# A two-layer hybrid decoder trunk in float32: the GLU projections moved to the head of the layer, the convolution wholly on VectorE, the indexer's head pairs scored one per unit

## The reference

```python
h = rms_norm(x, norm1_g[l])
proj = h @ w_in[l]
q, k, v, iq, ik, iw, glu_in, mq, gates = jnp.split(proj, bounds, axis=-1)
# A: index[q, s] = sum_h iw[h] * relu(iq_h . ik_s); top 64 keys per query; attention of 8 heads over those
# B: a, gte = split(glu_in + conv_in_b); u = a * sigmoid(gte)
#    causal depthwise convolution of u, 31 taps over 512 channels; LayerNorm; silu
# C: 4 heads of cross-attention into 256 memory tokens
merged = g[:, :, 0] * y_attn + g[:, :, 1] * y_mem + g[:, :, 2] * y_conv
x = x + merged @ w_out[l]
x = x + jnp.square(jax.nn.relu(rms_norm(x, norm2_g[l]) @ w_up[l])) @ w_down[l]
```

## Time and profile before

| | |
|---|---|
| Median of three runs | 2966.69 us (2966.26 to 2967.82) |
| The profiled execution's own time | 2967.76 us |
| Its span, first to last instruction | 2966.1 us |
| PE / DVE / ACT / POOL busy | 97% / 59% / 45% / 11% of the span |
| Mean granted clock of PE | 0.996 of full speed |
| Chain that ended last | PE 88%, DVE 5%, of it line 1152 (`conv_acc`) 3% |
| Idle of PE before line 548, released by DVE's `lo` | 37.3 us |
| Steps of the convolution on DVE (line 1152) | 180 of 707 ns mean |
| POOL's two kinds (lines 1578, 1580) | 60 of 1226 ns, 60 of 1057 ns |

### The profile page before, as it was taken

How to read it: one execution, slowest core, us unless ns; L and a number is a source line. 1 busy time by engine, 2 the same in 40 slices (tenths; PEclk the granted TensorE clock), 3 DMA queues, 4 the chain that set the end, 5 groups by cost and what they waited for, 6 DMA issues and landing times.

```text
span 2966.1 us, 38416 instructions
## 1 busy us (share of the span) xinstructions
PE 2891.1 (97%) x13120; PEld 2376.0 (80%) x13120; DVE 1745.2 (59%) x1849; ACT 1347.8 (45%) x1657; POOL 313.6 (11%) x331
## 2 busy tenths in 40 slices
PE   7998999999999999999999989999999999999998
PEld 6876788888888888888878768888888888888887
DVE  4689655556555555545546986555555555555554
ACT  5543644444443444444445446444444434344443
POOL 1158200000000000000020772000000000000000
PEclk9999999999999999999999999999999999999999
DMA  7653556665656556565565444666566565555653
GB/s 268 203 167 128 157 181 202 206 219 199 199 185 198 185 187 195 184 189 188 185 225 171 163 141 154 188 208 231 185 203 201 188 189 186 195 184 186 196 185 128
DMA packets 274090, 558.65 MB, mean 188 GB/s; under 512 B 13168, under 2 KB 13168, under 8 KB 271376
## 3 DMA queue, kind: packets, MB, share of 16 engines
q1 hardware_dynamic: 266384, 523.53, 53.8%
q0 software_dynamic: 5888, 30.02, 3.6%
q10 hardware_dynamic: 1664, 3.15, 0.3%
HBM read 550.37 MB, written 6.29 MB: 188 GB/s over the span
## 4 chain that ended last, share of the span: by engine, by line
PE 88%; DVE 5%; issue 4%; DMA 1%; ACT 1%; DVEq 0%; ACTq 0%; POOL 0%; POOLq 0%; SPq 0%
PE acc L548 28%; PE acc L550 28%; PE acc L549 28%; DVE conv_acc L1152 3%; PE tp L561 3%; DVE lo L1091 1%; ACT hi L818 1%; PE tp L631 1%; DMA conv_bias<-in_conv_o_b 1%; PE sc L615 0%; PE sc L604 0%; DVE index L1170 0%; DMA x_tok<-in_x 0%; DMA raw<-in_w_in 0%; DVE head_sum L1278 0%
## 5 line engine op out<-in xcount | busy, mean ns | idle before, releaser
L1091 DVE TENSOR_TENSOR lo<-raw,hi 128x1024 fp32r<-128x1024 f32 (+1 forms) x1008 | 1239.5, 1232 | 1172.4 <-ACT hi L818 1163.6
L818 ACT ACTIVATE hi<-raw 128x1024 fp32r<-128x1024 f32 (+1 forms) x1008 | 1055.6, 1048 | 1472.3 <-PE acc L550 1468.3
L548 PE MATMUL acc<-hi,hT_hi 128*128 128x512 f32 x2304 | 922.4, 400 | 37.3 <-DVE lo L1091 37.2
L550 PE MATMUL acc<-hi,hT_lo 128*128 128x512 f32 x2304 | 902.2, 392 | 0.0
L549 PE MATMUL acc<-lo,hT_hi 128*128 128x512 f32 x2304 | 901.2, 391 | 0.0
L548 PE MATMUL acc<-hi,bT_hi 128*128 128x512 f32 x1408 | 555.3, 394 | 0.0
L550 PE MATMUL acc<-hi,bT_lo 128*128 128x512 f32 x1408 | 548.9, 390 | 0.0
L549 PE MATMUL acc<-lo,bT_hi 128*128 128x512 f32 x1408 | 548.2, 389 | 0.0
L548 PEld LDWEIGHTS acc<-hi,hT_hi 128*128 128x128 f32 x2304 | 434.8, 189 | 135.6 <-DVE lo L1091 48.5
L550 PEld LDWEIGHTS acc<-hi,hT_lo 128*128 128x128 f32 x2304 | 434.6, 189 | 93.8
L549 PEld LDWEIGHTS acc<-lo,hT_hi 128*128 128x128 f32 x2304 | 435.1, 189 | 86.7
(11 more groups left out here) (224 smaller groups left out, 1641.1 us busy)
## 6 DMA issues: line engine op xcount, KB each, us to landing
raw<-in_w_in SPq DMA_DIRECT2D x160, 1024.0 KB, 5.0
raw<-in_w_up SPq DMA_DIRECT2D x128, 1024.0 KB, 5.3
raw<-in_w_down SPq DMA_DIRECT2D x128, 1024.0 KB, 5.1
raw<-in_w_out SPq DMA_DIRECT2D x32, 1024.0 KB, 5.1
raw<-in_w_mem_kv SPq DMA_DIRECT2D x16, 1024.0 KB, 5.1
raw<-in_w_attn_o SPq DMA_DIRECT2D x16, 1024.0 KB, 5.1
raw<-in_w_conv_o SPq DMA_DIRECT2D x8, 1024.0 KB, 5.0
raw<-in_w_mem_o SPq DMA_DIRECT2D x8, 1024.0 KB, 5.1
```

The costliest lines, as they stand in the source:

```text
L548: pe.matmul(o, a1, w1, start=first and dk == 0, stop=False)
L550: mm = pe.matmul(o, a2, w1, start=False, stop=last and dk == 1)
L818: act.activation(hi[:, u % 4, :, 0:w], raw[:, c, 2 * (u % 2):2 * (u % 2) + 2, 0:w], ACT.Copy).then_inc(hi_ready, 1)
L1091: dve.tensor_tensor(lo[:, u % 4, :, 0:w], raw[:, u // 2, 2 * (u % 2):2 * (u % 2) + 2, 0:w], hi[:, u % 4, :, 0:w].bitcast(F32), ALU.subtrac ...
```

## The change

The GLU groups become groups 0 and 1. All that hangs on them moves ahead by 24 units (`GLU_A_TAKEN` 36 to 12, `CONV_IN_FILL` 45 to 21), the indexer's groups and their side work go back by 16 units, and the short `IKW` group goes from units 8 to 15 to units 24 to 31. The taps, the GLU bias and the head gains are loaded by POOL at the very head of the layer's body, ahead of its wait for the squares, and the taps are turned at unit 6 (33 before). The convolution is all on DVE: four tiles, 124 steps over units 27 to 91, three to a unit but one on units that have other work. The eight indexer pairs stand on units 49 to 52 and 54 to 57 (36, 38, ... 50 before), the top-k rounds on 62, 65, ... 83 (58 to 79 before).

```diff
-(G_IQ0, G_IKW, G_IQ1, G_GLUA, G_GLUG, G_MK, G_MV, G_MQ, G_KV, G_Q0, G_Q1) = range(FRONT)
+(G_GLUA, G_GLUG, G_IQ0, G_IKW, G_IQ1, G_MK, G_MV, G_MQ, G_KV, G_Q0, G_Q1) = range(FRONT)
...
-INDEX_PAIR_AT = [36 + 2 * j for j in range(IDX_HEADS // 2)]
+INDEX_PAIR_AT = [49, 50, 51, 52, 54, 55, 56, 57]
...
-DVE_TILES = 3
-CONV_AT = 56
-
-DVE_CONV = [(51, 1), (52, 1), (53, 1), (54, 1), (55, 1)] + [(n, 2 + n % 2) for n in range(56, 92)]
-TOPK_AT = 58
+TOPK_AT = 62
+C_TILES = CONV // P
+CONV_AT, CONV_END = 27, 92
+
+CONV_SHARE = {n: 1 for n in [36, *range(31, 35), *range(42, 46), *range(53, 62), 69, 77, 83, 84, 85, 87, 89]}
+CONV_SHARE |= {TOPK_AT + 3 * r: 1 for r in range(TOPK // 8)}
+DVE_CONV = [(n, CONV_SHARE.get(n, 3)) for n in range(CONV_AT, CONV_END)]
...
                         if i == 0:
                             pe.wait_ge(conv_done, here.next("conv_done"))
-                            pe.wait_ge(conv_rest, here.next("conv_rest"))
...
-                for i in range(done, min(done + dict(DVE_CONV).get(n, 0), TAPS * DVE_TILES)):
-                    k, c = divmod(i, DVE_TILES)
+                for i in range(done, min(done + dict(DVE_CONV).get(n, 0), TAPS * C_TILES)):
+                    k, c = divmod(i, C_TILES)
...
-                k = n - CONV_AT
-                if k in range(TAPS):
-                    c = DVE_TILES
...
-                        link(pool.tensor_scalar(tap_part[:, :], uT[:, c, k:k + SEQ], tapT[:, c, k:k + 1], None,
-                                                ALU.mult))
-                        ins = pool.tensor_tensor(conv_acc[:, c], conv_acc[:, c], tap_part[:, :], ALU.add)
...
+                pool.dma_start(tap_rows[0:TAPS, :], conv_w[l]).then_inc(front_in, 16)
+                pool.dma_start(tap_rows[TAPS:TAPS + 1, :], conv_b[l].unsqueeze(0)).then_inc(front_in, 16)
+                pool.dma_start(glu_b[:, :, :], rows(v_glu_b[l])).then_inc(front_in, 16)
+                for i, g in enumerate((q_norm_g, k_norm_g, mq_norm_g, mk_norm_g)):
+                    pool.dma_start(head_gain[:, i], rows(g[l])).then_inc(front_in, 16)
+
                 pool.wait_ge(squared, here.now("squared") + T * CB)
```

More of the change, by code:

```diff
@@ L66 @@
 CHUNKS = 4
-(G_IQ0, G_IKW, G_IQ1, G_GLUA, G_GLUG, G_MK, G_MV, G_MQ, G_KV, G_Q0, G_Q1) = range(FRONT)
-PAIR = {g: i % 2 for i, g in enumerate((G_IQ1, G_GLUA, G_GLUG, G_MK, G_MV, G_MQ, G_KV, G_Q0, G_Q1))} | {G_IQ0: 1}
+(G_GLUA, G_GLUG, G_IQ0, G_IKW, G_IQ1, G_MK, G_MV, G_MQ, G_KV, G_Q0, G_Q1) = range(FRONT)
+PAIR = {g: 1 - i % 2 for i, g in enumerate(
+    (G_GLUA, G_GLUG, G_IQ0, G_IQ1, G_MK, G_MV, G_MQ, G_KV, G_Q0, G_Q1))}
 GROUPS = FRONT + 4 * CB + CB + 2 * FFN // COL
@@ L88 @@
 MEM_FILL = [[27, 28, 29, 30], [38, 39, 40, 41]]
-TAPS_FILL = 33
+TAPS_FILL = 6
 MEM_LOAD = 16
-IKW_FILL = [20, 21]
-IK_FILL = 28
-IQ_FILL = [[16, 17], [31, 32]]
-INDEX_PAIR_AT = [36 + 2 * j for j in range(IDX_HEADS // 2)]
+IKW_FILL = [36, 37]
+IK_FILL = 44
+IQ_FILL = [[32, 33], [48, 49]]
+INDEX_PAIR_AT = [49, 50, 51, 52, 54, 55, 56, 57]
 SEEN = [slice(SEQ, SEQ + P), slice(0, SEQ)]
 SEEN_KEYS = SEQ + P
-CONV_IN_FILL = [45, 46]
+CONV_IN_FILL = [21, 22]
 MK_FILL = [57, 58]
@@ L137, in fills_until @@
     return [f[1:] for f in FILLS].index(name) + 1
-IKW_TAKEN, IQ_TAKEN = 19, [12, 27]
+IKW_TAKEN, IQ_TAKEN = 35, [28, 43]
 X_SQUARES, X_MEAN = 5, 6
 MEM_SQUARES, MEM_SCALED, MEM_MEAN = [24, 35], [25, 36], 36
-GLU_A_TAKEN, GLU_G_TAKEN, GLU_TANH = 36, 43, 44
+GLU_A_TAKEN, GLU_G_TAKEN, GLU_TANH = 12, 19, 20
 ROWS_TAKEN = [52, 68, 76, 83, 91]
 MV_TAKEN = 60
-MASK_FREE = 60
+MASK_FREE = 62
 LN_STATS, LN_APPLY, Y_TANH = 99, 100, 103
@@ L176 @@
 }
-assert sum(count for _, count in DVE_CONV) >= TAPS * DVE_TILES
+assert sum(count for _, count in DVE_CONV) >= TAPS * C_TILES
 class Place:
@@ L272, in build @@
         y_tok = at("y_tok", [P, T, CONV], X + 6 * kb)
-        tap_part = at("tap_part", [P, SEQ], X + 10 * kb)
         y_tanh = at("y_tanh", [P, T, CONV], X + 12 * kb)
@@ L692, in side @@
                     if j == 0:
-                        emptied(("ik", 0, 0), ("iq", 1, 1))
+                        emptied(("ik", 0, 0))
+                    if j == IDX_HEADS // 4:
+                        emptied(("iq", 1, 1))
                     index_pair(j)
@@ L1506, in side @@
                     pool.dma_start(wide[:, :], mem_tokens[0]).then_inc(mem_in, 16)
-                    pool.dma_start(tap_rows[0:TAPS, :], conv_w[l]).then_inc(front_in, 16)
-                    pool.dma_start(tap_rows[TAPS:TAPS + 1, :], conv_b[l].unsqueeze(0)).then_inc(front_in, 16)
-                    pool.dma_start(glu_b[:, :, :], rows(v_glu_b[l])).then_inc(front_in, 16)
-                    for i, g in enumerate((q_norm_g, k_norm_g, mq_norm_g, mk_norm_g)):
-                        pool.dma_start(head_gain[:, i], rows(g[l])).then_inc(front_in, 16)
                 if n == MEM_MEAN + 1:
@@ L1528, in side @@
                     pair = PAIR[(G_IQ0, G_IQ1)[i]]
-                    pool.wait_ge(acc_free[pair], here.now(f"acc{pair}") + 2)
+                    pool.wait_ge(acc_free[pair], here.now(f"acc{pair}") + 3)
                     alone()
```

23 lines of the change are left out of this document (5 added, 18 removed).

## The result

The changed kernel takes 2952.47 us (median of 6 runs, 2947.87 to 2955.39); the kernel before took 2967.16 measured along with it (6 runs, 2966.23 to 2968.26). The ratio is 0.995, 95% interval 0.9937 to 0.9963. So it is faster by 14.7 us, about 0.5%, which is more than the 0.2% that a measurement of this kernel can tell. The forecast was 2942; the range, 2928 to 2960, held the time. The profiled execution took 2951.17 us, 16.6 less than the profiled one of before.

The account below looks back on a forecast made before the run. PE was taken to be held by VectorE, losing 25.6 us per layer in units 62 to 91. Per layer -25.6 + 6.6 + 6 = -13.0; two layers -26, start +1: -25, giving 2942 us, range 2928 to 2960.

Parts of the forecast that it names:

- What bounds the kernel and the step's length: PE waits for VectorE in units 62 to 91; without GpSimd's neighbouring work convolution steps average about 0.48 us.
- The load of 76 us: VectorE's work over units 62 to 90 falls from 102 to 76 us, against about 88 for PE.
- Units 62 to 91: PE loses 25.6 us per layer there; all goes but 6.6, a gain of 19.0.
- The third rival: Convolution steps stay long, at a mean of 0.71 us, so the kernel gets slower: 2975 us; chance 0.09.
- The condition I gave for being wrong: VectorE still busy throughout units 62 to 91, or PE losing over 10 us per layer ahead of unit 50.
- The heads' chain keeps 6.6: Attention heads' waits of 2.4, 2.4 and 1.8 us per layer stay, since no step of their loop is shortened.
- the first rival: The heads' chain waits were only VectorE's lateness and go as well: 2929 us; chance 0.18.
- Fills at units 29 and 30: New PE waits at the third and fourth memory-token fills, 2.6 and 1.0 us, together 3.6 per layer.
- At the second half PE waits 1.3: Second half of the memory tokens: PE waits 1.3 us per layer at its fill at unit 40.
- The clock: Granted clock is 0.98 to 1.00 of full speed in both stretches, so it takes no part; no term.
- My bounds for the front: New waits around the memory tokens, units 24 to 42: 6 us per layer, between 0 and 12.
- Second rival: GpSimd's rotations beside convolution steps at units 41 to 45 cost VectorE and PE 9 us per layer: 2960 us; chance 0.15.

Follow-up runs that it names:

- experiment 1: The kernel before with GpSimd's convolution tile left out except its first tap, VectorE's 93 steps unmoved: 2938.25 us.
- Experiments 7 and 8: 7: changed kernel computing 16 of 31 taps, 2937.83 us; 8: changed kernel with GpSimd normalising only 4 of each head's 128 columns, 2940.99 us.
- Experiment 4: The changed kernel with no convolution steps on the short units 27 to 30, moved to units 42 to 45 and the end: 2942.01 us.
- Experiments 2 and 9: 2: changed kernel's order with the convolution as before, 2972.18 us; 9: changed kernel with one step, not three, on units 35 and 37 to 41, 2944.55 us.
- the convolution alone: The kernel before, its order kept, with all four convolution tiles on VectorE over units 51 to 89: 2964.01 us.
- The joined kernel: Changed kernel with memory-token fills at 15 to 18 and 32 to 35, no steps on units 27 to 30 and 84 to 91, one on 36 to 39: 2935.11 us.

## Why the prediction was right in sign and 10 us off in size

**What bounds the kernel and the step's length: right.** PE was held by VectorE in units 62 to 91, and the neighbour made the steps long (experiment 1). Three steps take 1.27 us nearly everywhere. The mean of 543 ns lies above the forecast's 0.48, since a few runs beside the normalisation take 3 to 4 us. The load of 76 us that I gave VectorE for units 62 to 90 was too low: it is busy 82.5 us there.

**Units 62 to 91: right.** -19.9 us in the first layer against -19.0; without the clock it is -18.2 and -18.3 in the two layers. The third rival (a pitch that stays, 2975) fell with the step's mean. The condition I gave for being wrong, VectorE busy throughout this stretch, didn't come: the waits for `lo` are 1.5 us, under the 3 forecast.

**"The heads' chain keeps 6.6": the size nearly held, the reason was wrong.** By pace 25.6 - 19.9 = 5.7 us stay in the first layer (of the 25.6, 1.7 were clock); by waits it is 2.4 + 1.1 + 1.5 = 5.0, `s_buf` being gone and `lo` not. I argued that none of the chain's steps is shortened, so its waits stay. None is shortened (9.9 us in every kernel), but a wait depends on when the chain starts, and that is set by VectorE's lateness. Experiments 7 and 8 removed these waits without touching the chain. So the first rival named the right mechanism. It failed on the change itself, since GpSimd's multiplications of rows still hold VectorE up, which I had called covered: beside them one step took 2.12 us (at 226.41) and two runs of three 3.25 and 3.89.

**Fills at units 29 and 30: right.** 3.6 forecast, 4.0 measured (3.25 and 0.78). Experiment 4 takes the twelve steps away, and 0.7 us is left. One part of the 4.0 us I had not counted: GpSimd's rotation of the first indexer queries (95.79 to 100.07 us) now stands beside units 28 to 30 of VectorE, whose steps and splits take about 1.4 us more beside it (a run of three 1.71 for 1.27, two splits of 128x160 0.62 for 0.32).

**"At the second half PE waits 1.3": the term that was mis-sized.** It is 3.0. PE doesn't wait at the fill, as I had counted, but one step later: unit 40 is the first that multiplies the memory tokens, and needs the low part that VectorE takes at unit 42 behind its steps. VectorE also stood idle 6.67 us for ScalarE at unit 36, where I took 5.61 from before. Experiments 2 and 9 place the cause: the steps on units 35 to 41. Per layer the waits are 7.0 where I summed 6 with handovers; 2 us over both layers.

**The clock: missing from the sum.** I wrote that it takes no part, from windows of before. That was a misreading: the 0.98 of its stage from 210 to 350 us holds the piece at 294 us and the start of the one at 348 us named above. After has 10.2 us more at the 1.2 GHz level than before (27.3 - 17.1), which is 5.1 us. With the 2 us of waits above it makes 7 of the 8.4 us by which the profiled 2951.2 us lie above the 2942.8 of my sum. In the front of the layers it is 6.8 us in the first and 10.2 in the second more than before, so 3.4 and 5.1 us lost. With the waits (7.0 less 0.5 us in the first; 13.6 less 6.2, the start of the layer with them, in the second) that is 9.9 and 12.5, against +9.7 and +13.25 in the stretches. My bounds for the front, 0 to 12 us per layer, hold the first and miss the second by 1. So the range held the time, but not because it had a term for the clock.

**Second rival: refuted in size.** GpSimd's small rotations beside the steps cost VectorE little: three steps took 1.41 us for 1.27 at unit 41, a split 1.52 for 1.22 two units later, under 1 us in units 41 to 45, and with the 1.4 us at units 28 to 30 some 2 us per layer, where the rival had 9.

What stays open is why, of two stalls of 3 us, one is followed by half clock and the other not, and with it some 2 to 3 us of the difference between several of these kernels that waits and clock do not add up to (5 to 6 us between after and either before or the convolution alone, the two kernels in which VectorE is late most of the stage from unit 62 to 91).

## What to carry to other kernels

When work is taken from one engine and spread over another, price each unit in which it lands against the lead that the buffers allow there: here one half of the change alone gained 3.5 us and the other lost 4.7, the two together gained 15, and a few steps and fills shifted by some units another 17 to 20. A wait at the end of a chain of fixed length says when the chain started; look for what made its first step late before calling it the chain's own. Add to a new stall of PE what the clock takes after it, from a place in the trace where one did.

## What the hardware showed that I had not expected

A stall of PE of 3.25 us was followed by some 6.8 us at the 1.2 GHz level, one of 3.02 us in the first layer by none. The joined kernel stalls 3.07 us, and the window around it reads 1.00:

```profile
90.00:130.00 40.00, 36.00 (x196) 30.26 (x195) 30.27 (x50) 21.86 (x38) 7.59 (x12) 1.00 0.65 214
```

In the kernel before, waits of 1.16 and 1.55 us within 3 us of each other (the second layer, 1762 to 1764 us) were followed by 3.4 us of it as well.

Beside a GpSimd multiplication of 128x1024, three steps of VectorE took 3.89 us for 1.27, while its operations of 128x16 and 128x128 (0.2 to 1.7 us each) cost a VectorE instruction beside them at most 0.3 us, and one of 2.6 us on 128x8 nothing.
